# Order of ScalarE's work in the recurrent scan: the reloaded keys of the next-but-one pair behind the copies of turned keys

## The chip, the cores and the metric

The kernel runs on one core of one Trainium2 chip. The metric is device time in microseconds for one execution. Before the change three runs took 2662.40, 2662.72 and 2663.43 us, a median of 2662.72 us.

## What the reference computes

The reference is a two-layer transformer over 512 latent and 256 context tokens of width 1024, all in float32. Layer 0 mixes tokens by neighbourhood attention and a long convolution. Layer 1 mixes them by a recurrence (RWKV-7) with 16 heads of 64 channels, run forward and backward. Each layer ends with a gated feed-forward block. The change touches the recurrence alone. Cut to what matters:

```python
kk = rw_heads(k * k_k)
kk = kk / maximum(sqrt(sum(square(kk), -1)), 1e-12)
k_dir = k[None] * (1.0 + (a - 1.0) * k_a)           # per direction

def update(s, w_t, k_t, v_t, kk_t, a_t):             # s: 64 x 64 per head
    sa = einsum('ebhvk,ebhk->ebhv', s, kk_t)
    return s * w_t - sa (x) (kk_t * a_t) + v_t (x) k_t

s, ys = lax.scan(step, s0, ...)                      # 256 context tokens, then 512 latent ones
```

Then y is normed per head, a bonus term is added, and the result is gated and projected.

## The kernel before

The program is one block with a queue of instructions for each engine, and semaphores between them. Sections of layer 0, the feed-forward blocks and the projections run ahead of the scan and behind it. The scan (`scan_sp`, `scan_pool`, `scan_pe`, `scan_act`, `scan_dve`, lines 2013 to 2777) starts some 1570 us into the span and ends near 2150 us.

**Chunks.** The 768 tokens are cut into 12 chunks of 64. Inside a chunk the recurrence is turned into matrix products and the inverse of a triangular matrix; between chunks ten short products carry the 64x64 state along. Heads are taken in eight pairs, 0 to 7, since two heads of 64 channels fill 128 partitions. Both directions (`e` = 0, 1) of a pair are done together.

**Rounds.** `ROUNDS` holds triples (i, n, c) with n = i + 1 and c = i + 2, for i from -2 to 7. A round works on three pairs at once: it finishes pair i (inverse, transitions, chain of states, output), does the middle part of pair n (decays, scores, turned keys), and begins pair c (reload of keys, their norm). Six rounds, i = 0 to 5, have all three pairs. In round -1 there is no i, and in round 6 there is no c.

**Order.** Nothing reorders the work: each engine carries out its queue in the order in which the loop writes it, with the parts of i, n and c interleaved by hand. `AC`, `DV`, `PEM` and `PO` are lists of marks, one for each signalling instruction of ScalarE, VectorE, TensorE and GpSimd. A mark's place in the list is the value of that engine's semaphore that others wait for, so the lists must agree with the order in the queues.

**PSUM banks.** TensorE's products for n and c take turns in two pairs of banks (`front_bank`). A product may start when the one two turns before it has been taken out of its banks (`front`, the table `FRONT_FREE`). The turns that matter are tV, tB_0, tB_1, tK_0, tK_1, KD_0, CK_0, KD_1, CK_1, kk, BV_0, BV_1, kr.

The names, as they stand in the queues:

- tV, tB_0, tB_1, tK_0, tK_1 are transposes of six 128x128 blocks (L2153 on TensorE) and their copies from PSUM to SBUF by ScalarE (`tokens`, L2464). tK_e are the decayed keys of direction e of pair n.
- KD_e (`gram_keys`, L2191), CK_e (`gram_rest`, L2203) and BV_e (`value_gram`, L2215) are products of pair n. VectorE masks KD_e (mK, mD: L2623, L2625) and CK_e (mC, mL: L2632, L2634).
- c_1 to c_10 (`chain`, L2302) are the steps that carry the state of pair i from chunk to chunk, each followed by VectorE's st (L2667).
- kc (L2514) scales the keys of pair c, which SyncE's queue reloads from DRAM into `KDIR` (L2052) once VectorE's accr (L2735) of pair n is done. ksq (L2516) squares them, kk (`turned_sums`, L2292) sums the squares per head, kroot (L2522) takes the root.
- w16 (`squares`, L2162) is the first product of the next round. It waits for inverted 16x16 blocks that GpSimd works out (L2103, L2104) and that travel through DRAM (L2066, L2072).
- mean, var, vr and kr close the round. Behind them the next round begins with w16.
- st_1 to st_10, acc_1 (L2729) and accr (L2735) are VectorE's; accr stands behind st_2, and the masks of KD and CK stand between st_6 and st_10.

In TensorE's queue the part of a round around the change reads:

```text
tB_0, c_2, tB_1, c_3, tK_0, c_4, tK_1, c_5, KD_0, c_6, CK_0, c_7, KD_1, c_8, CK_1, c_9, kk, c_10, BV_0, ys, BV_1, ...
```

and in ScalarE's queue:

```text
tV, tB_0, tB_1 (n) | kc, ksq (c) | tK_0, tK_1 (n) | kroot (c) | bv_0 (n) | kwide (c) | ys (i) | bv_1 (n) | ...
```

Of the kernel before, what the change touches and what calls it, by code (L numbers as in the profile page):

```python
# [88 lines left out]
def hybrid_dit_kernel(nc, a, out):  # L89
# [3 lines left out]
    with ctx:  # L93
# [1791 lines left out]
        TOKK, KINT, BVT, XY, OO, MT, NE = carve(ARENA[3], [2 * T, 2 * T, 2 * T, 4 * T, 4 * T, 2 * T, 2 * T])  # L1885
# [50 lines left out]
        class Marks(dict):  # L1936
# [31 lines left out]
            (2, "kmax krec"), (0, "cen"), (2, "kmul"), (0, "rec f1 f2 z")))  # L1968
        AC = Marks(act_done, (
# [3 lines left out]
        PO = Marks(pool_done, ((1, "s00 s10 s01 s11 zero sub turn"),))  # L1973

# [26 lines left out]
        def here(n):  # L2001
            return 0 <= n < CT
# [436 lines left out]
        def scan_act(act):  # L2439

            def tangent(n, e, k):
                act.wait_ge(pe_done, PEM[f"l{e}{k}", n])
                AC.done(nc.scalar.activation(as_halves((SG, AA)[k][e]), halves(front_bank(f"l{e}{k}", n)), ACT.Tanh,  # L2443
                                             scale=0.5, bias=pcol((PW0, PA0)[k] + e, n)), f"t{e}{k}", n)

            def decays(n, e):
                act.wait_ge(dve_done, DV[f"scan_{e}", n])
                AC.done(nc.scalar.activation(SG[e], SU[e], ACT.Exp, scale=-DEC0), f"ep_{e}", n)
                AC.done(nc.scalar.activation(SU[e], SU[e], ACT.Exp, scale=DEC0), f"en_{e}", n)
                chunked = lambda x: x.rearrange("p (j t) -> p j t", t=TC)  # L2450
                last, first = ((TC - 1, 0), (0, TC - 1))[e]
                act.wait_ge(act_done, AC[f"ep_{e}", n])
                AC.done(nc.scalar.activation(ENDS[:, n % 2, e, :].unsqueeze(2), chunked(SG[e])[:, :, last:last + 1], ACT.Copy),
                        f"ends_{e}", n)
                act.wait_ge(pool_done, PO[f"s{e}1", n])
                AC.done(nc.scalar.activation(KT[e], AA[e], ACT.Identity, scale=pcol(PKA, n), bias=KA1[:, n:n + 1]),
                        f"rate_{e}", n)
                act.wait_ge(dve_done, DV["kmul", n])
                AC.done(nc.scalar.activation(chunked(KIN[e])[:, :, first:first + 1], chunked(KK)[:, :, first:first + 1],
                                             ACT.Copy), f"first_{e}", n)  # L2460

            def tokens(n, name, dst):
                act.wait_ge(pe_done, PEM[name, n])
                AC.done(nc.scalar.activation(dst.rearrange("p (g k) c -> p g k c", g=2),  # L2464
                                             halves(front_bank(name, n)).rearrange("p g (k c) -> p g k c", k=3), ACT.Copy),
                        name, n)

            def turned(n, e):
                act.wait_ge(pe_done, PEM[f"kT_{e}", n])
                b = front_bank(f"kT_{e}", n)  # L2470
                for k in range(2):
                    last = nc.scalar.activation(KINT[:, e, :, 3 * k:3 * k + 3, :],
                                                PS[:, b + k, 0:HALF].rearrange("p (j h t) -> p h j t", j=3, h=2), ACT.Copy)
                AC.done(last, f"kT_{e}", n)

            def paired(b):
                return PS[:, b:b + 2, 0:HALF]

            def solved(i, name, dst, src):
                act.wait_ge(pe_done, PEM[name, i])  # L2480
                AC.done(nc.scalar.activation(dst, src, ACT.Copy, scale=-1.0), name, i)

            flat = OO.rearrange("p e h j o t -> p e h (j o t)")
            act.wait_ge(cols_halved, 2)
            for i, n, c in ROUNDS:
                if here(n):
                    for e in range(2):
                        tangent(n, e, 1)
                    for e in range(2):
                        decays(n, e)  # L2490
                if here(i):
                    for e in range(2):
                        b = back_bank(f"oo_{e}")
                        solved(i, f"oo_{e}", flat[:, e, :, 0:512], PS[:, b:b + 2, :])
                    b = back_bank("oo_2")
                    solved(i, "oo_2", flat[:, :, :, 512:768],
                           PS[:, b:b + 2, :].rearrange("p h (e x) -> p e h x", e=2))
                if here(n):
                    turned(n, 0)
                    act.wait_ge(dve_done, DV["kd_0", n])  # L2500
                    AC.done(nc.scalar.activation(ACC[:, n % 2, :], KT[0][:, 0:L], ACT.Copy, scale=pcol(PRK, n)), "acc_0", n)
                if here(i):
                    act.wait_ge(pe_done, PEM["cg", i])
                    AC.done(nc.scalar.activation(GTS, PS[:, front_bank("cg", i) + 1, 0:L], ACT.Copy), "gt", i)
                if here(n):
                    turned(n, 1)
                    tokens(n, "tV", VTT)
                    tokens(n, "tB_0", TOKB[:, 0])
                    tokens(n, "tB_1", TOKB[:, 1])
                if here(c):  # L2510
                    act.wait_ge(keys_in, 32 * c + 32)
                    if c:
                        act.wait_ge(dve_done, DV["ba_1", n])
                    AC.done(nc.scalar.activation(KK, KDIR, ACT.Copy, scale=pcol(PKK, c)), "kc", c)  # L2514
                    act.wait_ge(act_done, AC["kc", c])
                    AC.done(nc.scalar.activation(KS, KK, ACT.Square), "ksq", c)  # L2516
                if here(n):
                    tokens(n, "tK_0", TOKK[:, 0])
                    tokens(n, "tK_1", TOKK[:, 1])
                if here(c):  # L2520
                    act.wait_ge(pe_done, PEM["kk", c])
                    AC.done(nc.scalar.activation(KROOT, PS[:, front_bank("kk", c), 0:12], ACT.Sqrt), "kroot", c)  # L2522
                if here(n):
                    act.wait_ge(pe_done, PEM["BV_0", n])
                    AC.done(nc.scalar.activation(BVT[:, 0].rearrange("p h j t -> p h (j t)"),
                                                 paired(front_bank("BV_0", n)), ACT.Copy), "bv_0", n)
                if here(c):
                    act.wait_ge(dve_done, DV["krec", c])
                    AC.done(nc.scalar.activation(KS.rearrange("p (k t) -> p k t", t=TC),
                                                 KROOT.unsqueeze(2).broadcast_to([128, 12, TC]), ACT.Copy), "kwide", c)  # L2530
                if here(i):
                    act.wait_ge(pe_done, PEM["ys", i])
                    AC.done(nc.scalar.activation(YS.rearrange("p (j w t) -> p w j t", w=2, t=TC),
                                                 PS[:, 2:4, 0:256].rearrange("p w (j t) -> p w j t", t=TC), ACT.Copy),
                            "ys", i)
                if here(n):
                    act.wait_ge(pe_done, PEM["BV_1", n])
                    AC.done(nc.scalar.activation(BVT[:, 1].rearrange("p h j t -> p h (j t)"),
                                                 paired(front_bank("BV_1", n)), ACT.Copy), "bv_1", n)
                if here(i):  # L2540
                    act.wait_ge(dve_done, DV["cen", i])
                    AC.done(nc.scalar.activation(FIN, YS, ACT.Square), "sq", i)
                    act.wait_ge(pe_done, PEM["var", i])
                    AC.done(nc.scalar.activation(VROOT, PS[:, 3, 0:8], ACT.Sqrt, scale=1.0 / CH, bias=small[:, 3:4]),
                            "groot", i)
                    act.wait_ge(dve_done, DV["rec", i])
                    AC.done(nc.scalar.activation(FIN.rearrange("p (k t) -> p k t", t=TC),
                                                 VROOT.unsqueeze(2).broadcast_to([128, 8, TC]), ACT.Copy), "vwide", i)
                if here(c):
                    for e in range(2):  # L2550
                        tangent(c, e, 0)
# [451 lines left out]
```

## Time and profile before

| | value |
|---|---|
| median of three runs | 2662.72 us |
| the profiled execution | 2657.89 us |
| its span, first to last instruction | 2656.1 us |
| mean granted TensorE clock | 0.929 of full speed |
| TensorE busy | 2331.5 us (88%) |
| VectorE busy | 939.2 us (35%) |
| GpSimd busy | 853.9 us (32%) |
| ScalarE busy | 665.1 us (25%) |

All times in the views are microseconds from the start of the span. In a row of the timeline the first number is the start and the second the duration of the merged instructions; a bracket says how long the engine was idle before and who ended that. A granted clock of 1.00 is 2.4 GHz and 0.50 is 1.2 GHz.

### The profile page before, as it was taken

To read this page: it belongs to the slowest core of one execution; us is meant where nothing else is said; L and a number is where in the kernel's file an instruction comes from. 1 tells how busy PE (TensorE), PEld (TensorE's weight loads), DVE (VectorE), ACT (ScalarE), POOL (GpSimd) and SP (SyncE) were. 2 spreads that over 40 slices of the span, in tenths; PEclk is the share of its full clock that TensorE was granted. 3 is DMA by queue.
4 is the path that set the end of the run, shared out by engine and by line. 5 is a ranking of instruction groups with operands and counts; after the bars stand their busy time and mean duration, and the time that the engine had idled before them with its cause. 6 is when DMAs were issued, how large, how long until landed. Compare 5 with 4: busy or idle time off the path is not lost. (4 is left out here: it accounts for less than half of the span.)

```text
span 2656.1 us, 50263 instructions
## 1 busy us (share of the span) xinstructions
PE 2331.5 (88%) x22240; PEld 1950.3 (73%) x22240; DVE 939.2 (35%) x1475; ACT 665.1 (25%) x1032; POOL 853.9 (32%) x699
## 2 busy tenths in 40 slices
PE   5899977989699999999579966888888957999997
PEld 3687754555399999999439956777777845788786
DVE  3100066890410000113584106666666632200123
ACT  4100165421320000122222114344333312211112
POOL 2123200100134444344034423333333314466562
PEclk8899988999799999999779988999999978999998
DMA  5555520002021112111113431111211112222231
GB/s 214 220 204 207 196 68 17 0 1 72 24 64 61 58 62 63 64 64 56 26 64 100 113 105 39 40 40 40 40 38 39 23 65 64 79 95 95 91 99 64
DMA packets 139266, 204.06 MB, mean 77 GB/s; under 512 B 87783, under 2 KB 97511, under 8 KB 131912
## 3 DMA queue, kind: packets, MB, share of 16 engines
q1 hardware_dynamic: 139080, 201.26, 24.1%
q8 instruction: 155, 2.54, 0.4%
q14 instruction: 31, 0.25, 0.0%
HBM read 183.93 MB, written 17.30 MB: 76 GB/s over the span
## 5 line engine op out<-in xcount | busy, mean ns | idle before, releaser
L258 POOL CAST TMP_r<-WR 128x1024 fp32r<-128x1024 f32 x120 | 126.1, 1051 | 753.0 <-DMA WR<-in_ffn_w_dram 436.5
L277 PE MATMUL PS<-H_r,TMP_r 128*128 128x384 f32 (+1 forms) x1088 | 331.8, 360 | 13.7 <-DVE Y_r L492 13.7
L277 PE MATMUL PS<-Y_r,TMP_r 128*128 128x384 f32 (+1 forms) x1088 | 328.9, 357 | 3.7 <-DVE H_r L492 3.7
L260 POOL TENSOR_TENSOR WR_r<-WR,TMP_r 128x1024 fp32r<-128x1024 f32 x120 | 288.8, 2407 | 9.6
L415 DVE TENSOR_TENSOR P<-TMP,PS 128x768 f32 (+1 forms) x44 | 36.1, 821 | 561.0 <-PE PS L277 561.0
L277 PEld LDWEIGHTS PS<-H_r,TMP_r 128*128 128x128 f32 x1088 | 202.3, 190 | 31.0 <-DVE Y_r L492 15.6
L277 PEld LDWEIGHTS PS<-Y_r,TMP_r 128*128 128x128 f32 x1088 | 202.0, 190 | 19.8 <-DVE H_r L492 4.0
L277 PE MATMUL PS<-H_r,WR_r 128*128 128x384 f32 x736 | 192.1, 343 | 0.0
L268 POOL CAST TMP_r<-WR 128x1024 fp32r<-128x1024 f32 x68 | 84.2, 1238 | 322.0 <-DMA WR<-in_rw_w_rkv_dram 167.0
L270 POOL TENSOR_TENSOR WR_r<-WR,TMP_r 128x1024 fp32r<-128x1024 f32 x68 | 165.8, 2439 | 5.4
L398 ACT ACTIVATE TMP<-PS 128x768 f32<-128x768 f32 (+1 forms) x44 | 31.1, 706 | 524.6 <-PE PS L277 524.6
L588 PE MATMUL PS<-H_r,TMP_r 128*128 128x384 f32 x704 | 151.9, 338 | 3.2 <-DVE H_r L626 2.2
L277 PE MATMUL PS<-Y_r,WR_r 128*128 128x512 f32 x352 | 139.0, 395 | 0.0
L277 PEld LDWEIGHTS PS<-H_r,WR_r 128*128 128x128 f32 x736 | 134.0, 190 | 0.0
L588 PEld LDWEIGHTS PS<-H_r,TMP_r 128*128 128x128 f32 x704 | 125.5, 189 | 3.8 <-DVE P L415 2.5
L1731 PE MATMUL PS<-P_r,TMP_r 128*128 128x384 f32 (+1 forms) x448 | 113.0, 344 | 0.3 <-DVE X_r L1856 0.3
L588 PE MATMUL PS<-Y_r,TMP_r 128*128 128x512 f32 x352 | 109.7, 393 | 2.1 <-DVE Y_r L626 2.1
L2085 POOL TENSOR_SCALAR scan_front<-scan_front 128x768 f32<-128x768 f32 x32 | 38.8, 1230 | 198.8 <-ACT scan_front L2443 198.8
L1622 PE MATMUL PS<-H_r,TMP_r 128*128 128x384 f32 x352 | 94.4, 350 | 8.7 <-POOL WR_r L260 8.5
L1622 PE MATMUL PS<-H_r,WR_r 128*128 128x384 f32 x352 | 92.1, 343 | 0.0
L1622 PE MATMUL PS<-Y_r,TMP_r 128*128 128x384 f32 x352 | 91.4, 341 | 0.0
L343 PE MATMUL PS<-Hraw,WR 128*128 128x384 f32 x256 | 85.5, 497 | 5.8 <-DVE Hraw L1425 5.8
(307 smaller groups left out, 4466.4 us busy)
## 6 DMA issues: line engine op xcount, KB each, us to landing
WR<-in_ffn_w_dram SPq DMA_DIRECT2D x88, 512.0 KB, 3.6
TMP<-in_mod_w_dram SPq DMA_DIRECT2D x40, 1024.0 KB, 4.9
WR<-in_down_dram SPq DMA_DIRECT2D x44, 512.0 KB, 3.5
WR<-in_mix_w_in_dram SPq DMA_DIRECT2D x24, 512.0 KB, 7.1
WR<-in_rw_w_rkv_dram SPq DMA_DIRECT2D x24, 512.0 KB, 4.2
P<-in_mod_w_dram SPq DMA_DIRECT2D x4, 2048.0 KB, 22.1
vkr_dram<-extra SPq DMA_DIRECT2D x16, 384.0 KB, 4.8
scan_front<-vkr_dram SPq DMA_DIRECT2D x16, 384.0 KB, 4.0
```

Source lines behind the costliest of these rows:

```text
L258: nc.gpsimd.tensor_copy(hi, raw).then_inc(weights_hi, 1)
L260: nc.gpsimd.tensor_tensor(lo, raw, hi.bitcast(F32), ALU.subtract).then_inc(weights_split, 1)
L268: nc.gpsimd.tensor_copy(hi, raw).then_inc(weights_hi, 1)
L270: nc.gpsimd.tensor_tensor(lo, raw, hi.bitcast(F32), ALU.subtract).then_inc(weights_split, 1)
L277: last = nc.tensor.matmul(PS[:, bank + b, 0:h1 - h0], w, x[:, h0:h1], start=k + p == 0, stop=k == CT - 1 and p == 2)
L343: last = nc.tensor.matmul(PS[:, 2 * s + h, 0:HALF], WR[:, s, k, :], outproj.rhs(k)[:, HALF * h:HALF * h + HALF], start=k == 0, stop=k == C ...
L398: nc.scalar.activation(as_halves(GATE[:, u, 0:d.n], d.n), halves(bank, d.n), ACT.Silu)\
L415: nc.vector.tensor_tensor(as_halves(dst, d.n), as_halves(GATE[:, u, 0:d.n], d.n), halves(4 * u + 2, d.n), ALU.mult).then_inc(d.unit_free, 1)
L588: last = nc.tensor.matmul(PS[:, bank, 0:h1 - h0], w[:, at:at + 128], x[:, q % 4, h0:h1], start=k + p == 0, stop=k == FT - 1 and p == 2)
L1622: last = nc.tensor.matmul(PS[:, 2 * u + b, 0:HALF], w, x[:, HALF * b:HALF * b + HALF], start=k + p == 0, stop=k == CT - 1 and p == 2)
L1731: last = nc.tensor.matmul(PS[:, 2 * (t % SLOTS) + b, 0:h1 - h0], wt, x[:, k, h0:h1], start=k + p == 0, stop=k == CT - 1 and p == 2)
L2085: PO.done(nc.gpsimd.tensor_scalar(x, x, 0.5, 0.5, ALU.mult, ALU.add), f"s{e}{k}", n)
```

## The change

ScalarE's copies tK_0 and tK_1 of pair n are written ahead of kc and ksq of pair c. The list of ScalarE's marks follows. No instruction is added, removed or altered, and the queues of the other engines stay as they are.

```diff
-            (0, "oo_0 oo_1 oo_2"), (1, "kT_0 acc_0"), (0, "gt"), (1, "kT_1 tV tB_0 tB_1"), (2, "kc ksq"), (1, "tK_0 tK_1"),
+            (0, "oo_0 oo_1 oo_2"), (1, "kT_0 acc_0"), (0, "gt"), (1, "kT_1 tV tB_0 tB_1 tK_0 tK_1"), (2, "kc ksq"),
...
                     tokens(n, "tB_1", TOKB[:, 1])
+                if here(n):
+                    tokens(n, "tK_0", TOKK[:, 0])
+                    tokens(n, "tK_1", TOKK[:, 1])
                 if here(c):
                     act.wait_ge(keys_in, 32 * c + 32)
                     if c:
...
                     AC.done(nc.scalar.activation(KS, KK, ACT.Square), "ksq", c)
-                if here(n):
-                    tokens(n, "tK_0", TOKK[:, 0])
-                    tokens(n, "tK_1", TOKK[:, 1])
                 if here(c):
                     act.wait_ge(pe_done, PEM["kk", c])
```

## Rows read from the trace of the kernel before

**Rows 1.** The stages: scan; busy PE, PEld, DVE, ACT, POOL, clock, DMA share, GB/s.

```profile
1560.00:2140.00 580.00, 481.49 (x12241) 417.67 (x12243) 351.65 (x557) 219.63 (x317) 173.78 (x304) 0.92 0.19 39
```

**Rows 2.** Who waited for whom, 1560 to 2150: total, times, longest.

```profile
ACT scan_front L2514 <- DMA scan_front<-vkr_dram: 37.9, 8, 11.2
PE PS L2191 <- ACT scan_back L2464: 32.3, 7, 8.7
```

**Rows 3.** Timeline of SyncE's reload and ScalarE, round 1.

```profile
1748.15 0.34 SPq L2052 DMA_DIRECT2D scan_front<-vkr_dram  x1
...
1751.95 0.94 ACT L2514 ACTIVATE scan_front<-scan_front,PC 128x768 f32<-128x768 f32 x1 [3.18 <-DMA scan_front<-vkr_dram]
1752.92 0.84 ACT L2516 ACTIVATE scan_front<-scan_front 128x768 f32<-128x768 f32 x1
1753.67 1.49 ACT L2464 ACTIVATE scan_back<-PS 128x768 f32<-128x768 f32 x2
```

**Rows 4.** Timeline of TensorE, round 1: tK_0, c_5, KD_0, kk, BV_0.

```profile
1748.23 0.88 PE L2153 MATMUL PS<-ident,scan_front 128*128 128x128 f32 x6
...
1750.22 0.45 PE L2302 MATMUL PS<-scan_back 64*64 64x64 f32 x8
1754.51 1.98 PE L2191 MATMUL PS<-scan_tokens,scan_front 64*64 64x128 f32 x32 [3.84 <-ACT scan_back L2464]
...
1761.75 1.50 PE L2292 MATMUL PS<-scan_front 128*128 128x2 f32 x12 [0.65 <-DVE scan_tokens L2625]
...
1763.46 1.57 PE L2215 MATMUL PS<-scan_tokens,scan_front 64*64 64x64 f32 x48
```

**Rows 5.** A stretch of round 1, columns as in rows 1.

```profile
1754.50:1756.50 2.00, 1.99 (x39) 1.99 (x41) 0.00 (x0) 1.95 (x2) 1.62 (x6) 0.50 0.00 0
```

**Rows 6.** Timeline, round 6 (no pair c): tK_0, KD_0 and VectorE's mD_1.

```profile
2095.93 0.88 PE L2153 MATMUL PS<-ident,scan_front 128*128 128x128 f32 x6
...
2098.20 1.04 PE L2191 MATMUL PS<-scan_tokens,scan_front 64*64 64x128 f32 x30
...
2103.37 0.68 DVE L2625 TENSOR_TENSOR scan_tokens<-PS,extra 128x512 f32<-128x512 f32 x1
```

**Rows 7.** A stretch of round 6, columns as in rows 1.

```profile
2098.40:2100.00 1.60, 1.60 (x88) 1.60 (x80) 0.97 (x5) 0.43 (x1) 1.32 (x4) 1.00 0.00 0
```

**Rows 8.** Timeline of TensorE: tK_0 and BV_0 in rounds 0, 3, 5.

```profile
1678.26 0.87 PE L2153 MATMUL PS<-ident,scan_front 128*128 128x128 f32 x6
1693.27 1.96 PE L2215 MATMUL PS<-scan_tokens,scan_front 64*64 64x64 f32 x48
...
1886.75 0.88 PE L2153 MATMUL PS<-ident,scan_front 128*128 128x128 f32 x6
1902.98 1.57 PE L2215 MATMUL PS<-scan_tokens,scan_front 64*64 64x64 f32 x48
...
2026.21 0.87 PE L2153 MATMUL PS<-ident,scan_front 128*128 128x128 f32 x6
2041.10 1.57 PE L2215 MATMUL PS<-scan_tokens,scan_front 64*64 64x64 f32 x48
```

**Rows 9.** Timeline of TensorE, round -1 and the start of round 0.

```profile
1618.70 1.99 PE L2191 MATMUL PS<-scan_tokens,scan_front 64*64 64x128 f32 x32 [8.68 <-ACT scan_back L2464]
...
1636.49 4.42 PE L2162 MATMUL PS<-scan_back,scan_tokens 64*64 64x64 f32 x96 [3.39 <-DMA scan_back<-inv_dram]
```

**Rows 10.** Source view of L2072, round 3: issues, landing; then w16 (timeline).

```profile
L2072 SPq DMA_DIRECT2D scan_back<-inv_dram x8: 303/528/1705, 1897.9 to 1903.4; - x8
...
DMA to landing us min/median/max: 3.2/4.1/4.2
...
1915.01 2.95 PE L2162 MATMUL PS<-scan_back,scan_tokens 64*64 64x64 f32 x93
```

**Rows 11.** Timeline of GpSimd, round 1: equal shapes, first beside VectorE's L2729.

```profile
1746.45 0.91 POOL L2104 TENSOR_TENSOR scan_small<-scan_small 96x120 f32<-96x120 f32 x1
...
1751.57 0.43 POOL L2104 TENSOR_TENSOR scan_small<-scan_small 96x120 f32<-96x120 f32 x1
```

## The prediction

> **What bounds the kernel now.** I read the busy time by stage first. In the scan TensorE is busy 481 of 580 us, at a mean clock of 0.92, and no other engine more than 352 [rows 1]. So the scan ends when TensorE's queue ends, and what counts is where that queue stands still. The view of waits comes second: TensorE waits 32.3 us, in seven places, at KD_0 for ScalarE's copy of tK_0, and ScalarE itself waits 37.9 us at kc for the reload of keys, in eight places [rows 2]. The reader should see one stall in these two lines. The timelines of round 1 show it whole: SyncE issues the reload at 1748.15; ScalarE, done with tB_1, waits 3.18 us for it at kc (1751.95), then squares (1752.92), and only then copies tK_0 and tK_1 (1753.67) [rows 3]. TensorE had made tK_0 from 1748.23 on and reached the end of c_5 at 1750.67; KD_0 needs the banks that tK_0 holds and starts at 1754.51 after 3.84 us of nothing [rows 4]. Behind KD_0 in TensorE's queue stand c_6 to c_10, so the chain of states, and with it VectorE, stands still too.
>
> The stall costs more than its length. Right behind it the granted clock is 0.50, the 1.2 GHz level, and KD_0 takes 1.98 us [rows 4, 5]. Round 6 has no pair c, hence no kc, and shows the same products without the stall: 30 of KD_0's 32 products take 1.04 us, at a clock of 1.00 (2.4 GHz) [rows 6, 7]. That round is the model for all others after the change.
>
> **The change part by part.** It removes nothing and adds nothing. Two copies move ahead of kc and ksq on ScalarE.
>
> tK_0's copy can start when TensorE has made it: 1748.23 and 0.88 give 1749.11 in round 1 [rows 4]. Two copies take 1.49 us [rows 3], and ScalarE is free at that time. So KD_0 finds its banks free about 1749.9, before c_5 ends at 1750.67, and does not wait. The copy of tK_1, behind tK_0's, is out by about 1751.2, before CK_0 needs those banks.
>
> What sets the pace then? In round 6 VectorE's masks: TensorE starts tK_0 at 2095.93, and mD_1, which frees the banks that kk needs, ends at 2103.37 and 0.68, so 2104.05. That is 8.12 us [rows 6]. A round with a pair c has kk too: add 0.1 us of hand-over (an estimate; the merged row of the copies puts the first one's end near 1754.4, and KD_0 starts at 1754.51 [rows 3, 4]) and the 1.71 us from kk to BV_0, 1761.75 to 1763.46 [rows 4]. tK_0 to BV_0 should take 8.12 + 0.1 + 1.71 = 9.93 us.
>
> Before, the same stretch takes, in rounds 0 to 5, 15.01, 15.23, 15.01, 16.23, 14.90 and 14.89 us; four of the six have their rows [rows 4, 8]. The sum is 91.27. Less 6 x 9.93 = 59.58 this is 31.7 us. Of it 23.6 us are the idle time itself (32.3 less the 8.68 of round -1 [rows 2, 9]); the other 8 us, 1.3 a round, are the slow clock behind it.
>
> Round -1 gives nothing. Its stall is the longest, 8.68 us, but the next round's w16 waits already 3.39 us for the inverted blocks from DRAM and starts at 1636.49 [rows 9]. Those come by VectorE's mA_1, GpSimd and SyncE, none of which waits for KD_0. An earlier end of round -1 only lengthens that wait. Bounds: a gain of 0, or a microsecond either way if the clock stands differently at w16.
>
> What the moved-back kc and ksq cost. They start when the keys land, at 1751.95 as before, since accr and SyncE's queue are unchanged, and ksq ends at 1753.76 [rows 3]. The copies that now go first are done before that, so kc is not pushed. First to need ksq is kk, now at 1748.23 + 8.22 = 1756.45: 2.7 us to spare. In round 3, where the keys are latest, I make it 2.0 us from the same view. Cover gone, each microsecond costs one, six times. Behind ksq only kroot stands, which waits for kk anyway. So this edit costs 0.
>
> What is late next. w16 of the next round also needs the inverted blocks. In round 3 the last of the eight transfers is issued at 1903.4 and lands at most 4.2 us later, 1907.6; w16 starts at 1915.01 [rows 10], and would start 6.3 us earlier, 1908.7. That leaves 1.1 us, the tightest of the six rounds by the same view (about 1.4 to 4 elsewhere). The next round's blocks move forward with their own round. I take no wait here; if the blocks were late by 1 to 3 us more, a round would give back about that less its spare.
>
> The remaining tail of a round (BV_0 to w16) is unchanged and moves forward as a whole; so do the transfers after the scan, which wait for the last z.
>
> **A rule against.** The view of stretches shows TensorE at 1.00 in KD_0 to c_7 of round 6, right behind five transposes [rows 6, 7]. The Trainium skill (TensorE: Matmul & The Clock Gate, Part 4: PE-mode transpose) says that transposes do not count as TensorE activity in the same way, so that the full clock does not engage for them. By that, KD_0 would still start at 1.2 GHz after the five transposes, and only the idle time would come back: 23.6 instead of 31.7 us. Round 6 speaks against it for these transposes.
>
> **The sum.** The profiled execution took 2657.89 us, its span 2656.1. 2657.89 - 31.7 = 2626.2. The median of the runs lies 4.83 above the profiled execution; I carry that over: 2631.0 us.
>
> **The rivals.**
> (a) The clock stays low, or falls elsewhere. The stall goes, but KD_0 to c_7 still run at 1.2 GHz, or the sparse end of a round now meets a drop that it did not before. For: the clock falls in several places of the scan (mean 0.92 [rows 1]). Against: round 6 at 1.00 [rows 7]. Gain 23.6 us, 2639 us.
> (b) The inverted blocks become the bound. The masks now run while GpSimd still works on them. A GpSimd instruction beside a VectorE one with both inputs in SBUF takes 0.91 instead of 0.43 us [rows 11]. Some nine GpSimd instructions of 0.25 to 0.45 us lie under the moved masks; doubled they cost about 3 us, of which about 1 is spare, so 2 a round come back: gain 20 us, 2643 us. Against: the masks read PSUM with one of their inputs, and round 6 had masks and GpSimd at the same time and its w16 did not wait.
> (c) Slower: the keys' wait moves from KD_0 to kk and grows. Place: TensorE's queue at kk, with c_10, BV_0, ys and BV_1 behind it. ksq would have to end later than kk's old start, 1761.75, which is 8.0 us later than now [rows 3, 4]; each microsecond beyond costs six. A reload 10 us later would give 2662.7 + 12 = 2675 us. For: at 384 KB a piece the reload is the largest transfer of the round. Against: nothing that it competes with has moved towards it.
> (d) The change does not do what it says: KD_0 waits for something else that ends at the same time (the operands of pair n, its other inputs). Then 2662.7 us. Against: the operands were there for tK_0 and tK_1 themselves, and round 6 starts KD_0 with no wait.
>
> **How the numbers follow.** Forecast 0.72, (a) 0.12, (b) 0.08, (c) 0.03, (d) 0.05. The forecast's own spread is some 4 us each way: the clock's drops at w16 and in round 0's BV_0 (1.96 against 1.57 us [rows 4, 8]) may fall otherwise, and runs differ by 1 us. The range takes in (a) and most of (b): 2625 to 2645. Runs of this kernel differ by 0.04%, so 0.2%, 5.3 us, is what can be told from no change. Faster: forecast, (a) and (b), 0.92, and a little of (d): 0.93. Same: 0.04. Slower: 0.03.
>
> **What would show it.** Right: in rounds 0 to 5 no idle time of TensorE before L2191, kc still released by the transfer, the copies of tK 4 us ahead of it, clock 1.00 from KD_0 to c_7, tK_0 to BV_0 in 9.9 us, kk released by L2625 as before. Round -1: w16 still at about 1636.5 behind a wait of about 10 us. Wrong: kk released by ksq in rounds 0 to 5 (c), w16 released by the transfer there (b), KD_0 at 1.98 us (a), or idle time before L2191 with another releaser (d).

## The result and the profile after

The changed kernel takes 2629.59 us (median of 4 runs, 2627.11 to 2634.23), the kernel before, run beside it, 2663.07 us (4 runs, 2662.40 to 2666.13). The ratio is 0.9881, with a 95% interval of 0.9865 to 0.9897. A second comparison gave 0.9881 again (0.9853 to 0.9909). That is 31.5 to 33.5 us; forecast were 31.7.

The profiled execution of the changed kernel took 2631.05 us, its span is 2629.3. Against the profiled one of before that is 26.8 us only; the difference between the two figures is explained below.

The stretches of the changed kernel, columns as in [rows 1]: TensorE is denser over the same 580 us. Behind it stand two stretches of round 1.

```profile
1560.00:2140.00 580.00, 498.27 (x12680) 429.56 (x12678) 359.42 (x582) 223.44 (x322) 171.03 (x304) 0.91 0.19 38
1744.00:1746.00 2.00, 2.00 (x96) 2.00 (x98) 1.07 (x5) 0.99 (x2) 1.69 (x5) 1.00 0.98 342
1753.00:1754.50 1.50, 1.50 (x34) 1.50 (x34) 0.23 (x1) 0.00 (x0) 0.00 (x0) 0.50 0.08 16
```

The second row answers to [rows 5]: KD_0 and CK_0 now run at 1.00. The third lies in BV_0: the clock is at 0.50 there, where before it stood at 1.00 in five of six rounds.

Who waited for whom, 1560 to 2150 (totals, times, longest; PEld is the loading of weights ahead of a product):

```profile
ACT scan_front L2517 <- DMA scan_front<-vkr_dram: 19.7, 8, 11.2
...
PE PS L2191 <- DVE scan_tokens L2625: 5.8, 8, 0.7
...
PEld PS L2191 <- ACT scan_back L2464: 0.3, 1, 0.3
```

These answer to [rows 2]. The row in which TensorE's products waited 32.3 us for ScalarE at L2191 is gone; 0.3 us are left for one weight load. What is left ahead of L2191 is VectorE's mask of the product two turns before, 5.8 us. ScalarE's own wait for the keys fell from 37.9 to 19.7 us, since it does its copies in that time; 11.2 of it are those of the first pair.

ScalarE and then TensorE in round 1 of the changed kernel (kc is now L2517 and ksq L2519):

```profile
1742.84 0.81 ACT L2464 ACTIVATE scan_back<-PS 128x768 f32<-128x768 f32 x1 [0.37 <-PE PS L2153]
1744.02 0.81 ACT L2464 ACTIVATE scan_back<-PS 128x768 f32<-128x768 f32 x1 [0.37 <-PE PS L2153]
1745.82 0.94 ACT L2517 ACTIVATE scan_front<-scan_front,PC 128x768 f32<-128x768 f32 x1 [0.98 <-DMA scan_front<-vkr_dram]
1746.79 0.84 ACT L2519 ACTIVATE scan_front<-scan_front 128x768 f32<-128x768 f32 x1
```

```profile
1741.93 0.87 PE L2153 MATMUL PS<-ident,scan_front 128*128 128x128 f32 x6
...
1744.20 1.04 PE L2191 MATMUL PS<-scan_tokens,scan_front 64*64 64x128 f32 x30
...
1750.54 1.50 PE L2292 MATMUL PS<-scan_front 128*128 128x2 f32 x12 [0.72 <-DVE scan_tokens L2625]
...
1752.35 2.78 PE L2215 MATMUL PS<-scan_tokens,scan_front 64*64 64x64 f32 x48
```

Against [rows 3, 4]: each copy follows its transpose, KD_0 starts 2.2 us behind tK_0's start instead of 6.3, with no idle time, and kk is held by VectorE's mask, not by ksq, which ends at 1747.63 with 2.9 us to spare (2.5 to 2.9 in rounds 0 to 5; in round -1 kk does wait for ksq, 1.72 us, and what follows shows that this costs nothing). BV_0 takes 2.78 us instead of 1.57: that is the low clock of the row above.

The ends of round -1 and of round 6, timeline of TensorE, w16 of the next round:

```profile
1634.97 5.04 PE L2162 MATMUL PS<-scan_back,scan_tokens 64*64 64x64 f32 x96 [11.37 <-DMA scan_back<-inv_dram]
...
2086.25 4.71 PE L2162 MATMUL PS<-scan_back,scan_tokens 64*64 64x64 f32 x96 [0.46 <-DMA scan_back<-inv_dram]
```

The first answers to [rows 9]: the wait has grown from 3.39 to 11.37 us and w16 starts where it did (1.5 us earlier in a scan that began 2 us earlier).

**Where the time came from.** The starts of w16 in round 0 and of w16 in round 6 bound the six rounds that changed: 1636.49 to 2053.54 before, 417.05 us, and 1634.97 to 2024.47 after, 389.50 us. From the starts in the two timelines, summed over the six rounds:

| part of a round | before | after | gained |
|---|---|---|---|
| tK_0 to BV_0 | 91.27 | 60.11 | 31.16 |
| BV_0 to BV_1 | 21.17 | 25.68 | -4.51 |
| all else (417.05 and 389.50 less the above) | 304.61 | 303.71 | 0.90 |
| w16 of round 0 to w16 of round 6 | 417.05 | 389.50 | 27.55 |

The first line is the forecast's sum, 31.7. The second is new: BV_0 to BV_1 took 4.8 us in one round before (round 0) and takes 4.7 to 4.8 in four after, against 3.27 in the others. Outside these six rounds the stretch ahead is 1.5 us shorter and the one behind 2.3 us longer, so 26.8 us are left of the 27.55.

### The profile page after: what moved, and what is told of

Its sections match the earlier page's. It is cut to its first block and busy times, and to the rows that moved or that the text cites. A ratio compares the mean times of both kernels' runs of the same rounds, so it can differ in the third digit from the quotient of the medians.

```text
span 2629.3 us, 50263 instructions
## 1 busy us (share of the span) xinstructions
PE 2328.6 (89%) x22240; PEld 1946.6 (74%) x22240; DVE 938.3 (36%) x1475; ACT 666.3 (25%) x1032; POOL 852.3 (32%) x699
## 5 line engine op out<-in xcount | busy, mean ns | idle before, releaser
L277 PE MATMUL PS<-H_r,WR_r 128*128 128x384 f32 x736 | 191.7, 342 | 0.0
L1622 PE MATMUL PS<-H_r,WR_r 128*128 128x384 f32 x352 | 92.1, 343 | 0.0
L588 PE MATMUL PS<-H_r,WR_r 128*128 128x384 f32 x352 | 90.9, 340 | 0.0
```

What stands on the lines that cost most here:

```text
L277: last = nc.tensor.matmul(PS[:, bank + b, 0:h1 - h0], w, x[:, h0:h1], start=k + p == 0, stop=k == CT - 1 and p == 2)
L588: last = nc.tensor.matmul(PS[:, bank, 0:h1 - h0], w[:, at:at + 128], x[:, q % 4, h0:h1], start=k + p == 0, stop=k == FT - 1 and p == 2)
L1622: last = nc.tensor.matmul(PS[:, 2 * u + b, 0:HALF], w, x[:, HALF * b:HALF * b + HALF], start=k + p == 0, stop=k == CT - 1 and p == 2)
```

## The experiments

The measure beside the ratio is the time from w16 of round 0 to w16 of round 6 in each kernel's trace (from here the six rounds), since it leaves out the layers ahead and behind. "Low" counts the rounds among the six in which BV_0 to BV_1 takes more than 4.3 us instead of 3.27. The kernel before ran beside each group of four: 2659.24 us for the first, 2656.09 for the second, 2659.76 for the third.

| kernel | median us | ratio to before (95%) | six rounds | low |
|---|---|---|---|---|
| before | 2663.07 | 1 | 417.05 | 1 |
| changed | 2629.59 | 0.9881 (0.9865 to 0.9897) | 389.50 | 4 |
| e1, tK_0 alone ahead | 2645.22 | 0.9953 (0.9937 to 0.9968) | 408.44 | 3 |
| e2, early reload, old order | 2632.44 | 0.9894 (0.9869 to 0.9918) | 394.60 | 2 |
| e3, stall filled, old order | 2649.72 | 0.9967 (0.9955 to 0.9979) | 409.51 | 2 |
| e4, round -1 alone | 2658.86 | 0.9998 (0.9984 to 1.0013) | 417.21 | 2 |
| e5, keys 1.8 us later | 2634.07 | 0.9926 (0.9907 to 0.9945) | 392.29 | 5 |
| e5, keys 5.6 us later | 2659.69 | 1.0013 (1.0003 to 1.0023) | 418.63 | 6 |
| e6, changed + 8 fillers | 2617.51 | 0.9855 (0.9838 to 0.9872) | 382.46 | 0 |
| e7, changed + early reload | 2627.42 | 0.9887 (0.9868 to 0.9907) | 393.37 | 5 |
| changed again | 2628.21 | 0.9881 (0.9853 to 0.9909) | 388.91 | 3 |
| e8, changed + 4 fillers | 2620.89 | 0.9855 (0.9826 to 0.9883) | 381.33 | 0 |
| e9, later keys + 8 fillers | 2624.73 | 0.9865 (0.9837 to 0.9893) | 385.11 | 1 |
| e10, early reload + 8 fillers | 2619.57 | 0.9846 (0.9816 to 0.9876) | 382.96 | 0 |

### e1: half of the change

```diff
                     tokens(n, "tB_1", TOKB[:, 1])
+                    tokens(n, "tK_0", TOKK[:, 0])
...
                     AC.done(nc.scalar.activation(KS, KK, ACT.Square), "ksq", c)
                 if here(n):
-                    tokens(n, "tK_0", TOKK[:, 0])
                     tokens(n, "tK_1", TOKK[:, 1])
```

> The change by half: tK_0 alone is copied ahead of kc, tK_1 stays behind ksq. My theory (TensorE's queue stops at the first product whose banks are not out): KD_0 starts right behind c_5 with no idle time, and the stall moves to CK_0, which needs the banks of tK_1; ksq still ends some 5.5 us behind tK_0's start, so CK_0 starts about 6.3 us behind it instead of 3.5 in the changed kernel. About 2 to 2.8 us a round are lost of the 5.3, so the gain is 15 to 20 us: 2643 to 2648 us. Rival (only KD_0's stall costs, CK_0 has slack because VectorE's masks set the pace): the same time as the changed kernel, 2630 us.

Measured: 12.5 us gained by the ratio (14 by the medians), where 15 to 20 were expected and the rival said 32. The stall moved as foreseen; timeline of TensorE, round 1:

```profile
1746.27 1.42 PE L2203 MATMUL PS<-scan_tokens,scan_front 64*64 64x64 f32 x48 [3.05 <-ACT scan_back L2464]
```

CK_0, not KD_0, now stands still, 3.05 us, and runs slower behind it. KD_0 to BV_0, summed over six rounds, takes 66.7 us against 47.2 in the changed kernel, 3.2 us a round and not 2 to 2.8. So both copies are needed: the queue stops at the first product whose banks are not out. What the copies hold is not the reason, since the first products that read it (L2259) come in the next round.

### e2: the same stall taken away at its other end

KDIR's last reader is kd_1, so its reload need not wait for accr. The new semaphore `rdir_in` carries the queries' reload.

```diff
-                        sp.wait_ge(dve_done, DV["accr", n])
+                        sp.wait_ge(dve_done, DV["kd_1", n])
                     sp.dma_start(KDIR, vkr_dram[1, c]).then_inc(keys_in, 16)
-                    sp.dma_start(RDIR, vkr_dram[2, c, :, 0:L]).then_inc(keys_in, 16)
+                    if c:
+                        sp.wait_ge(dve_done, DV["accr", n])
+                    sp.dma_start(RDIR, vkr_dram[2, c, :, 0:L]).then_inc(rdir_in, 16)
...
-                    act.wait_ge(keys_in, 32 * c + 32)
+                    act.wait_ge(keys_in, 16 * c + 16)
...
+                v.wait_ge(rdir_in, 16 * n + 16)
                 DV.done(nc.vector.tensor_tensor(RT[:, n % 2, e, :], RDIR, ...
```

> The old order on ScalarE, but the keys are reloaded as soon as their last reader kd_1 is done (about 6 us earlier), with a semaphore of their own; the queries' reload waits for accr as before. My theory (the stall is the reload's lateness seen through ScalarE's queue): kc finds its keys, kc and ksq take 1.8 us behind tB_1, so KD_0 waits only about 0.6 us; gain 26 to 29 us, 2634 to 2637 us, and the clock stays at 1.00 through KD_0. Rival (the order as such matters, two 0.9 us passes ahead of the copies are what holds TensorE): KD_0 still waits about 2 us or more a round, 2645 us or above.

Measured 28 us by the ratio, as expected. Timeline of ScalarE and then TensorE, round 1 (kc is L2517, ksq L2519, the copies L2467, KD_0 L2194):

```profile
1745.79 0.93 ACT L2517 ACTIVATE scan_front<-scan_front,PC 128x768 f32<-128x768 f32 x1
1746.75 0.84 ACT L2519 ACTIVATE scan_front<-scan_front 128x768 f32<-128x768 f32 x1
1747.50 1.49 ACT L2467 ACTIVATE scan_back<-PS 128x768 f32<-128x768 f32 x2
...
1748.34 1.10 PE L2194 MATMUL PS<-scan_tokens,scan_front 64*64 64x128 f32 x32 [0.55 <-ACT scan_back L2467]
```

kc finds its keys, and the two passes ahead of the copies make TensorE wait 0.55 us, not 3.84, in each of the six rounds. So the stall was the wait of kc, seen through ScalarE's queue. The order as such costs little: tK_0 to BV_0 takes 64.3 us in six rounds, 4.2 more than in the changed kernel.

### e3: the stall stays, the clock does not fall

```diff
+            def fill(count, step):
+                pe.wait_ge(dve_done, DV[f"st1_{step}", i])
+                for _ in range(count):
+                    nc.tensor.transpose(PS[:, 0, 256:384], ident[:, :], ident[:, :])
...
+                if here(i) and here(c):
+                    fill(24, 5)
                 if here(n):
                     gram_keys(n, 0)
```

> The old order, and in rounds 0 to 5 TensorE carries out 24 transposes of the identity into unused columns while it would stand still ahead of KD_0 (they wait for VectorE's st of chunk step 5, since they write its bank). The stall itself stays. My theory (about 8 of the 32 us are the half clock behind the stall): KD_0 now runs in 1.1 us at 1.00, tK_0 to BV_0 takes some 13.7 us instead of 15.2, gain 6 to 9 us, 2654 to 2657 us. Rival 1 (VectorE's masks set the pace whatever the clock): no gain, 2663 us. Rival 2 (transposes do not keep the clock up, as the Trainium skill says in TensorE: Matmul & The Clock Gate, Part 4: PE-mode transpose): KD_0 at 1.98 us and 0.50, 2663 us.

Measured: 8.8 us by the ratio, 7.5 in the six rounds. Timeline of TensorE in round 1 (the first row is tK_0), and the clock in the transposes and in KD_0:

```profile
1743.17 0.87 PE L2153 MATMUL PS<-ident,scan_front 128*128 128x128 f32 x6
...
1746.07 2.84 PE L2309 MATMUL PS<-ident 128*128 128x128 f32 x24 [0.46 <-DVE scan_back L2674]
1749.17 1.10 PE L2191 MATMUL PS<-scan_tokens,scan_front 64*64 64x128 f32 x32 [0.26 <-ACT scan_back L2471]
...
1746.10:1748.90 2.80, 2.80 (x24) 2.57 (x24) 0.00 (x0) 2.26 (x3) 2.33 (x7) 1.00 0.50 165
1749.20:1750.40 1.20, 1.20 (x49) 1.20 (x53) 0.00 (x0) 1.18 (x2) 0.94 (x4) 1.00 0.00 0
```

KD_0 still starts 6.0 us behind tK_0 (6.3 before), and takes 1.10 us at 1.00 instead of 1.98 at 0.50. tK_0 to BV_0 is 13.68 us (BV_0 starts at 1756.85), as expected, and 84.1 in six rounds against 91.27. So 7 to 8 of the 32 us are the clock, as the sum had it. It also speaks against the rule of the Trainium skill that the full clock does not engage for transposes (TensorE: Matmul & The Clock Gate, Part 4: PE-mode transpose): here TensorE did nothing but transposes for 2.84 us, and the clock stood at 1.00 in them and behind them.

### e4: the change in round -1 alone

```diff
+        AC = Marks(act_done, AC_OLD, AC_NEW, lambda it: it == -1)
...
+                if here(n) and (i == -1):
+                    tokens(n, "tK_0", TOKK[:, 0])
+                    tokens(n, "tK_1", TOKK[:, 1])
                 if here(c):
                     act.wait_ge(keys_in, 32 * c + 32)
...
-                if here(n):
+                if here(n) and not (i == -1):
                     tokens(n, "tK_0", TOKK[:, 0])
```

> The new order in round -1 alone, the old one in all others. My theory (round -1 ends in a wait for the inverted blocks from DRAM that does not depend on it): KD_0 of round -1 starts 8 us earlier, w16 of round 0 does not move, its wait for the transfer grows from 3.4 to about 11 us; 2663 us, within 1.5 us of the kernel before. Rival (the early end of round -1 lets the tangents and scans of pair 1 run ahead, so round 0 is shorter): 2 to 7 us faster.

Measured 0.9998, from 0.9984 to 1.0013. TensorE in rounds -1 and 0 (KD_0 is L2196, w16 L2167):

```profile
1609.44 1.10 PE L2196 MATMUL PS<-scan_tokens,scan_front 64*64 64x128 f32 x32 [0.20 <-ACT scan_back L2469]
...
1634.98 5.28 PE L2167 MATMUL PS<-scan_back,scan_tokens 64*64 64x64 f32 x94 [10.01 <-DMA scan_back<-inv_dram]
```

The longest single stall, 8.68 us, is worth nothing: it turned into wait for the transfer.

### e5: how much room the keys have now

```diff
                         sp.wait_ge(dve_done, DV["accr", n])
+                    if here(i):
+                        sp.wait_ge(dve_done, DV["st1_4", i])      # st1_7 in the second kernel
                     sp.dma_start(KDIR, vkr_dram[1, c]).then_inc(keys_in, 16)
```

> The changed kernel, with the reload of keys held back until VectorE's st of chunk step 4, about 1.8 us later than accr. My theory (after the change kk is the first to need ksq and has 2.9 us to spare in round 1, 2 or more in all): ksq ends about 1.1 us ahead of kk, no time lost, 2630 us (2627 to 2633). Rival (c) of the prediction (the wait for keys moved to kk and is as sharp there): 6 x 1.8 us more, 2641 us.

> As e5_late4, but held back until the st of chunk step 7, about 5.6 us later than accr. My theory: the spare 2.9 us are used up, ksq ends some 2.7 us after kk could start, and TensorE stands still ahead of kk for ksq; 6 x 2.7 = 16 us slower than the changed kernel, 2646 us, and more by up to 8 us if the clock falls behind that stall too. Rival (the keys are hidden whenever they come, since kroot and the norm are needed only in the next round): 2630 us.

The wait stands in SyncE's queue, so the reload of queries and what else comes behind the keys is held back with them.

With 1.8 us the ratio rose from 0.9881 to 0.9926, some 12 us, where none was expected; the trace shows 2.8 us more in the six rounds. The room was not as large as I had taken it. Timeline of TensorE, kk in round 3 and CK_1 in round 2:

```profile
1878.59 1.59 PE L2294 MATMUL PS<-scan_front 128*128 128x2 f32 x12 [0.81 <-ACT scan_front L2521]
...
1812.78 0.38 PE L2205 MATMUL PS<-scan_tokens,scan_front 64*64 64x64 f32 x9 [1.02 <-issue]
```

ksq ends 0.15 us ahead of kk in rounds 1 and 3 (0.6 to 1.8 us in the others), against 2.5 to 2.9 in the changed kernel: in these two rounds kc starts 2.4 and 2.7 us later behind tK_0, not 1.8. The wait is little longer than the one for the mask (0.5 to 0.7 us), so it cost some tenths. In rounds 0, 2 and 4 TensorE stopped in the middle of CK_1 for 0.85, 1.02 and 1.22 us, without a wait that the trace shows; neither trace of the changed kernel has such a stop. KD_0 to kk takes 1.9 us more in six rounds, kk to BV_1 1.4 more. What makes these stops, and the rest of the ratio's 12 us, stays open.

With 5.6 us all is lost, 35 us by the ratio, where 16 to 24 were expected. Timeline of round 1 (kc L2519, kk L2294) and the clock behind:

```profile
1753.34 0.93 ACT L2519 ACTIVATE scan_front<-scan_front,PC 128x768 f32<-128x768 f32 x1 [7.36 <-DMA scan_front<-vkr_dram]
...
1755.29 2.28 PE L2294 MATMUL PS<-scan_front 128*128 128x2 f32 x12 [4.55 <-ACT scan_front L2521]
...
1758.00:1762.00 4.00, 4.00 (x80) 4.00 (x79) 0.81 (x4) 1.20 (x2) 0.00 (x0) 0.50 0.75 73
```

kk starts 9.5 us behind KD_0 instead of 6.1, on the mean of six rounds: 3.4 us a round, 20 in all; kk to BV_1 takes another 8.5 us more, at half clock. That is 29 us in the six rounds (418.63 against 389.50). This is rival (c) of the prediction made true: the wait for keys moves to kk, where it costs about what it did at KD_0 (24.1 us of it cost 29.1 us here; 23.6 us cost 27.6 there).

### e6 and e8: the clock behind kk

```diff
+                if here(i) and here(c):
+                    fill(4, 6)                                     # e6 alone
                 if here(i):
                     chain(i, 7)
...
+                if here(i) and here(c):
+                    fill(4, 8)                                     # e6 and e8
                 if here(i):
                     chain(i, 9)
```

> The changed kernel, and in rounds 0 to 5 four transposes of the identity into unused columns ahead of c_7 and four ahead of c_9, where TensorE waits 0.5 to 0.7 us for VectorE's masks anyway. My theory (in four of six rounds of the changed kernel the clock falls to 0.50 right behind kk, since the stretch from c_7 to kk is thin, and BV_0 to BV_1 takes 4.8 instead of 3.3 us): fewer or no such drops, up to 6 us faster than the changed kernel, 2624 to 2629 us; kk starts no later. Rival (kk's twelve products of two columns alone let the clock fall, or it falls at random): as the changed kernel, 2630 us.

> The changed kernel with the four filling transposes ahead of c_9 alone. My theory (what decides is how thin TensorE's work is over the whole stretch from KD_0 to kk, so half the filling gives half the effect): 3 to 4 us faster than the changed kernel, against 7 with both, and some rounds with BV_0 at half clock are left. Rival (only the last gap ahead of kk counts): the full 7 us.

e6 is 7 us faster than the changed kernel (0.9855 against 0.9881, where up to 6 us were expected), and in all six rounds BV_0 to BV_1 takes 3.27 us. e8, with half the filling, does the same: my expectation of half the effect fell, its rival stood. The intervals of the ratios overlap, but in the last group e8's six runs (2619.32 to 2625.08 us) all lie below the changed kernel's six (2626.06 to 2633.26). Round 1 of e8, timeline of TensorE:

```profile
1743.29 0.65 PE L2309 MATMUL PS<-ident 128*128 128x128 f32 x4
1743.88 0.45 PE L2302 MATMUL PS<-scan_back 64*64 64x64 f32 x8
1744.26 1.50 PE L2292 MATMUL PS<-scan_front 128*128 128x2 f32 x12
...
1745.97 1.57 PE L2215 MATMUL PS<-scan_tokens,scan_front 64*64 64x64 f32 x48
```

Four transposes take the place of the 0.72 us in which TensorE waited for VectorE's mask ahead of kk, and BV_0 takes 1.57 us instead of 2.78. They are not quite free: KD_0 to kk takes about 0.2 us a round more.

### e7, e9, e10 and the changed kernel again: what adds up

> The new order and the earlier reload of keys together. My theory (with the new order nobody on the path waits for the keys in rounds 0 to 5; only kk of round -1 does, which is hidden behind the wait for the inverted blocks): the same as the changed kernel, 2630 us, within 2 us. Rival (the two gains add, since each removes a part of the other's wait): 2620 us or less.

> The changed kernel again, as the yardstick on the chip of the three others. Ratio to the kernel before 0.988, as measured for it, within 0.002.

> e5_late4 (keys 1.8 us later) with the filling transposes of e6_fillkk. My theory (the keys still had room there, and what e5_late4 lost, about 3 us in its trace and up to 10 in its median, was the clock behind kk): the filling gives it all back, the same as e6_fillkk within 2 us, ratio 0.985 to 0.986. Rival (the later keys cost time by themselves, through kk or SyncE's queue): 3 us or more slower than e6_fillkk, ratio 0.987 or above.

> New order, earlier reload of keys and filling transposes, all three. Theory: as e6_fillkk, ratio 0.985 to 0.986, since the keys are off the path. Rival (earlier transfers free the queue of SyncE or ScalarE for something late): 3 us or more faster than e6_fillkk.

e7 joins e2's edit to the changed kernel and gains nothing (0.9887 against 0.9881): the two edits remove one and the same wait. e10, with the fillers, equals e6 within its interval. e9 is e5's first kernel with the fillers: 0.9865, 2.7 us more than e6 in the six rounds, with one low round (1.55 us more) and one stop of 1.14 us that the trace puts down to TensorE's own issue; in the middle of CK_1 again. ksq ends 0.1 to 0.2 us ahead of kk in rounds 2, 3 and 4. I had expected the fillers to give back what the later keys cost, and they did not: the later keys cost 2.8 us in the six rounds without fillers (392.29 against 389.50) and 2.7 with them (385.11 against 382.46). So the traces do not show the clock as what they cost. The ratio's 12 us of e5 stay unexplained: the intervals of the groups (0.2% each) allow between 5 and 19, and with fillers the ratio puts the same delay at 2.7.

## Why the prediction was right

**The stall and its length.** Right: no idle time of TensorE for ScalarE ahead of KD_0 in rounds 0 to 5 (23.6 us before), and e1 and e2 show that the bank turn and kc's wait made it, not another input of KD_0. Rival (d) is out.

**The pace after it.** Round 6 as the model for the others held: tK_0 to BV_0 was put at 9.93 us and takes 9.89, 10.42, 9.90, 10.03, 9.90 and 9.97.

**The clock's share.** Put at 8 us; e3, which gives back the clock and leaves the stall, gained 7.2 us from tK_0 to BV_0, 7.5 in the six rounds and 8.8 by the ratio.

**Round -1 at nothing.** Right, and shown alone by e4.

**ksq's room.** Put at 2.7 us in round 1; the trace has 2.9. Put at 2.0 in round 3, where it is 2.6; the least is 2.5, in round 0. It is used up soon: with the reload issued 1.8 us later ksq came last ahead of kk in two rounds (e5).

**The inverted blocks.** In rounds 0 to 5 they were in time, as forecast, so rival (b) did not come. But w16 behind round 6 waited 0.46 us, a round that the working had left out, since it has no pair c: its own period is the same as before, but its masks and transfers came closer.

**What was mis-sized.** Rival (a) had said that the clock may fall elsewhere, at the sparse end of a round, and it did, with the stall gone as well: a low BV_0 in four rounds instead of one, 4.5 us in the profiled execution. The forecast had named BV_0's drop, in round 0, as a source of spread and put nothing for it into the sum; e6 and e8 show what it costs. It accounts for most of the 4.9 us between the forecast gain of 31.7 and the 26.8 of the two profiled executions.

**Luck in the number.** The forecast took 2626.2 us for the profiled execution and added 4.83, the distance of the earlier median from the earlier profile, which gave 2631.0. The profiled execution took 2631.05, and the median, 2629.59, lies 1.46 below it. So the two errors nearly cancel. Why the medians differ by 33.5 us where the profiles differ by 26.8 is not shown; low rounds, at 1.5 us each, are a part of the scatter. The forecast's "runs of this kernel differ by 0.04%" came from three runs: 26 further runs of the kernel before lie between 2651.08 and 2666.21 us, 11 others between 2650.33 and 2670.85.

## What to carry to other kernels

An engine that takes results out of banks should not stand at a transfer's wait ahead of a copy that another engine's queue needs; put the copy first, or start the transfer at its last reader; here the two cures were worth nearly the same and did not add (e2, e7). Count a stall of TensorE at its length plus the slow stretch behind it (here 3.9 and 1.3 us a round), which a few transposes in the idle time saved here (e3, e6, e8). And before a stall is priced, see who waits at the end of its round: the longest one here was worth nothing (e4).

## What the runs showed of the hardware that I had not expected

TensorE's clock fell to 0.50 in round 1 of the changed kernel with no idle time above 0.72 us ahead of it: what stood there were two such waits for masks and then twelve products of two columns each (kk, 1.50 us). With four 128x128 transposes ahead of c_9 it fell there in none of the six rounds, though kk was the same. The same kernel without them had 4 and 3 low rounds in two traces, and 5 in two near relatives (e5 with 1.8 us, e7), so where the clock falls in this stretch changes with the execution.
